# Narrow products in the recurrence levels and an early first expert in a one-core layer with attention, recurrence and experts

## The reference

```python
def hgrn_block(q, k, v, logf, S0):
    b = jnp.cumsum(logf, axis=1)
    diff = b[:, :, None] - b[:, None, :]
    decay = jnp.exp(jnp.where(causal[None, :, :, None, None], diff, -jnp.inf))
    A = jnp.einsum('bthk,btshk,bshk->bhts', q, decay, k)
    o = jnp.einsum('bhts,bshv->bthv', A, v) + jnp.einsum('bthk,bhkv->bthv', q * jnp.exp(b), S0)
    S_new = jnp.exp(bL)[..., None] * S0 + jnp.einsum('bshk,bshv->bhkv', k * jnp.exp(bL[:, None] - b), v)

def hier_moe(h, w_group, w_router, wg, wu, wd):
    g_sel = jnp.argmax(t @ w_group, axis=-1)
    top_v, top_i = lax.top_k(e_logits_of_the_group, 2)
    gates = p_group * jax.nn.softmax(top_v, axis=-1)
    experts = g_sel[:, None] * 8 + top_i
    # rows are sorted by expert and padded to blocks of 128; for each block xb of expert e:
    #   (silu(xb @ wg[e]) * (xb @ wu[e])) @ wd[e], times the gate, added to the token's row
```

## Time and profile before

| | |
|---|---|
| median of 3 runs | 2820.53 us (2820.53 to 2821.08) |
| the profiled execution | 2819.19 us, span 2817.5 us |
| TensorE busy | 2675.3 us (95%) |
| VectorE, ScalarE, GpSimd busy | 1548.5, 763.4, 713.5 us |
| DMA | 432.73 MB, mean 154 GB/s |
| projection and recurrence | about 10 to 1075 us |
| sample attention, then attention with routing | about 1075 to 1841 us |
| experts | about 1843 to 2817.5 us |

### The profile page before, as it was taken

The page is one execution under the profiler, slowest core; times in us unless marked ns, Lnnn a source line. Parts: engine busy times, 40 slices in busy tenths (PEclk is TensorE's granted clock), DMA queues, the critical chain, the costliest instruction groups (busy, mean ns, idle before and its releaser), DMA issues. The chain is left out here.

```text
span 2817.5 us, 38815 instructions
## 1 busy us (share of the span) xinstructions
PE 2675.3 (95%) x11801; PEld 1605.4 (57%) x11802; DVE 1548.5 (55%) x2861; ACT 763.4 (27%) x2102; POOL 713.5 (25%) x1001
## 2 busy tenths in 40 slices
PE   8999999999999987999999999759999999999996
PEld 6777777767777766455555555424444444444442
DVE  3565665555565565667777767625444444544443
ACT  1222222222222221555565666101111111111111
POOL 2111111111111120112222222133443433434332
PEclk9999999999999998899999999779999999999998
DMA  6000000100000029222212111389998878898883
GB/s 255 31 31 34 26 26 26 41 30 34 26 26 26 30 62 317 95 90 90 90 46 90 46 46 61 95 297 385 389 388 318 325 250 323 326 338 325 295 288 128
DMA packets 233641, 432.73 MB, mean 154 GB/s; under 512 B 31618, under 2 KB 89346, under 8 KB 233552
## 3 DMA queue, kind: packets, MB, share of 16 engines
q1 hardware_dynamic: 168080, 324.48, 32.2%
q0 software_dynamic: 30768, 94.78, 9.2%
q10 hardware_dynamic: 34704, 12.37, 1.7%
HBM read 324.77 MB, written 94.95 MB: 149 GB/s over the span
## 5 line engine op out<-in xcount | busy, mean ns | idle before, releaser
L673 PE MATMUL z_psum<-w_in_sb,hT 128*128 128x512 f32 x1088 | 482.1, 594 | 0.0
L667 PE MATMUL z_psum<-hT,w_in_sb 128*128 128x128 f32 x3264 | 374.2, 276 | 3.2 <-DMA w_in_sb<-in_w_in 3.2
L667 PEld LDWEIGHTS z_psum<-hT,w_in_sb 128*128 128x128 f32 x3264 | 370.0, 193 | 4.1 <-issue 4.1
L2081 PE MATMUL gate_psum<-w_gate_sb,block_rows_T 128*128 x720 | 318.9, 596 | 21.7 <-DMA w_gate_sb<-in_w_e_gate 21.7
L673 PEld LDWEIGHTS z_psum<-w_in_sb,hT 128*128 128x128 f32 x1088 | 200.4, 190 | 222.0 <-issue 221.0
L2085 PE MATMUL up_psum<-w_up_sb,block_rows_T 128*128 x720 | 316.4, 592 | 1.5 <-DMA w_up_sb<-in_w_e_up 1.5
L2095 PE MATMUL down_psum<-w_down_sb,hidden_T 128*128 x720 | 316.3, 592 | 0.4 <-DVE hidden_T L2003 0.4
L1274 ACT ACTIVATE w_in_sb<-score_psum,neg_max 128x512 f32<-128x512 f32 (+3 forms) x320 | 196.9, 622 | 203.1 <-DVE neg_max L1361 202.8
L310 POOL TENSOR_TENSOR level_decay<-log_decay 128x256 f32<-128x256 f32 x116 | 73.6, 634 | 702.9 <-DVE level_operand L505 702.9
L1948 ACT ACTIVATE square_out<-block_out 128x1024 f32<-128x1024 f32 x45 | 46.2, 1027 | 755.7 <-issue 738.9
L2081 PEld LDWEIGHTS gate_psum<-w_gate_sb,block_rows_T 128*128 128x128 f32 x720 | 137.4, 191 | 195.9 <-issue 195.9
(11 more groups left out here) (308 smaller groups left out, 3425.0 us busy)
## 6 DMA issues: line engine op xcount, KB each, us to landing
w_gate_sb<-in_w_e_gate SPq DMA_DIRECT2D x32, 2048.0 KB, 13.9
w_up_sb<-in_w_e_up SPq DMA_DIRECT2D x32, 2048.0 KB
w_down_sb<-in_w_e_down SPq DMA_DIRECT2D x32, 2048.0 KB, 12.5
w_in_sb<-in_w_in SPq DMA_DIRECT2D x7, 2048.0 KB, 18.7
hidden_by_lane<-hidden ACTq DMA_DIRECT2D x720, 16.0 KB
scratch_z<-z_ring SPq DMA_DIRECT2D x34, 256.0 KB, 2.0
scratch_y<-w_in_sb SPq DMA_DIRECT2D x17, 512.0 KB, 2.6
scratch_h<-h SPq DMA_DIRECT2D x17, 512.0 KB, 2.6
```

Source lines behind the costliest of these rows:

```text
L667: mm = pe.matmul(out[:, hd * P:(hd + 1) * P], w[:, g, c, hd * P:(hd + 1) * P], hT[:, u, c, :], start=(c == 0), stop=(c == DC - 1))
L673: mm = pe.matmul(out[:, :], hT[:, u, c, :], w[:, g, c, :], start=(c == 0), stop=(c == DC - 1))
L2081: mm = pe.matmul(gps[:, :], xT[:, u, c, :], part(wg, slot, c), start=(c == 0), stop=(c == DC - 1))
```

## The change

Levels 2 to 7 of the 16 prompt tiles stream only the 64 late (query) columns of each head; the results lie side by side in the first 64 columns of a head's bank. Level 2 loads 96 columns of weights and is merged by two plain copies of 32 partitions; levels 3 to 7 are merged by a masked copy of half the elements.

The expert stage's gate and up weights, gathered rows and gathered sums now lie in `w_in_sb` and their semaphores live across both stages. Expert 0 is always the first run (a one is written into the presence table). Its gate and up weights are loaded by SP behind the next-to-last tile's rows; the first 128 slots of its queue are read from the table, turned into row numbers on VectorE, and gathered by GpSimd before the stage ends. In `experts` these loads and this gather are gone, and the down weights of run 0 come behind gate and up of run 1. The gates are stored in three pieces: tiles 0 to 13 and the sample tile early, tiles 14 and 15 behind the arrival of the block lists.

```diff
@@ merge
+                if pos == 2 and not is_last(t):
+                    nc.vector.tensor_copy(heads(A[:, :])[0:32, :, 32:64], heads(lps[0][:, :])[0:32, :, 0:32])
+                    nc.vector.tensor_copy(heads(A[:, :])[64:96, :, 96:128], heads(lps[0][:, :])[64:96, :, 32:64]).then_inc(cp_ok, 1)
+                    return
+                if pos > 2 and not is_last(t):
+                    by_half = lambda a: a.rearrange("p h (g s m) -> p h g s m", s=2, m=m)[:, :, :, 1, :]
+                    nc.vector.copy_predicated(by_half(heads(A[:, :])), by_half(mask[:, l:l + 1, :].to_broadcast([P, HEADS, P])),
+                                              heads(lps[pos % 2][:, :])[:, :, 0:64].rearrange("p h (g m) -> p h g m", m=m)).then_inc(cp_ok, 1)
+                    return
@@ level
+                    elif pos == 2 and not is_last(t):
+                        mm = pe.matmul(lps[0][0:96, hd * P:hd * P + 64], left[:, hd * P:hd * P + 96],
+                                       halves_of(right[:, c], 32)[:, :, 1, :], start=True, stop=True)
+                    elif pos > 2 and not is_last(t):
+                        mm = pe.matmul(lps[pos % 2][:, hd * P:hd * P + 64], left[:, c],
+                                       halves_of(right[:, c], P >> pos)[:, :, 1, :], start=True, stop=True)
@@ attend_mix, SP
             store_y(LAST - 1)
             spread_h(LAST - 1)
+            sp.wait_ge(s_ps, FIRST[NU])
+            sp.dma_start(pre["wg"][:, 0, :, :], dr["w_e_gate"].rearrange("l e (c p) f -> (l e) p c f", p=P)[0]).then_inc(pre["g_in"], 16)
+            sp.wait_ge(pv, FIRST[NU])
+            sp.dma_start(pre["wu"][:, 0, :, :], dr["w_e_up"].rearrange("l e (c p) f -> (l e) p c f", p=P)[0]).then_inc(pre["u_in"], 16)
             store_y(LAST)
+            sp.wait_ge(gates_ok, 1)
+            for tiles in EARLY:
+                store_gates(tiles)
             sp.wait_ge(h_ok, TILES)
             sp.dma_start(h2[ORDER[LAST]], h[:, :]).then_inc(h_out, 16)
             sp.wait_ge(h_out, 16 * TILES)
-            sp.wait_ge(gates_ok, 1)
-            with nc.allow_non_contiguous_dma(reason="two gates for a token"):
-                sp.dma_start(dr["gates"][0:2 * TILES * P].rearrange("(t p c) o -> p t (c o)", p=P, c=2), gates[:, :, :]).then_inc(gates_out, 16)
+            sp.wait_ge(sc_out, 32 * TILES)
+            with nc.allow_non_contiguous_dma(reason="slots of the first block, one at a time"):
+                for j in range(LANES):
+                    sp.dma_start(keep["first_slots"][j * SQ:(j + 1) * SQ, :],
+                                 dr["table"][0].rearrange("(i r) o -> r (i o)", r=SQ)).then_inc(first_in, 16)
+            sp.wait_ge(blk_in, 16)
+            sp.wait_ge(gates_ok, 2)
+            store_gates(LATE)
@@ attend_mix, GpSimd, behind the fetch of block_queue_rows
+            pool.wait_ge(first_ok, 1)
+            pool.wait_ge(h_out, 16 * TILES)
+            for i in range(LANES):
+                pool.indirect_dma_start(out=pre["xg"][:, 0, i, :], out_offset=None, in_=dr["h2"].rearrange("t (j d) -> (t j) d", j=LANES),
+                                        in_offset=bass.IndirectOffsetOnAxis(ap=keep["first_rows"][:, i:i + 1], axis=0)).then_inc(pre["x_in"][0], 16)
@@ attend_mix, VectorE
+            chain.after(nc.vector.memset(full[:, 0, 0:1], 1.0))
...
+            dve.wait_ge(first_in, 16 * LANES)
+            chain.after(ts(keep["first_slots"][:, :], keep["first_slots"][:, :], 0.5, -0.25, ALU.mult, ALU.add))
+            ts(keep["first_rows"][:, :], keep["first_slots"][:, :], float(LANES), lane[:, 0:1], ALU.mult, ALU.add).then_inc(first_ok, 1)
             dve.wait_ge(blk_in, 16)
@@ experts, SP
-            gate(0)
-            up(0)
-            down(0)
             gate(1)
             up(1)
+            down(0)
@@ experts, GpSimd
-            gather(0, 0)
+            pool.sem_inc(tok_ok, 1)
             gather(1, 1)
@@ build
+            pre |= {"wg": w[:, 0:3, :, :], "wu": w[:, 3:6, :, :],
+                    "xg": w[:, 6, 4:8, :].rearrange("p c n -> p (c n)").rearrange("p (u i n) -> p u i n", u=2, i=LANES),
+                    "yg": w[:, 6, 0:4, :].rearrange("p c n -> p (c n)").rearrange("p (u d) -> p u d", u=2),
```

57 lines of the change are left out of this document (35 added, 22 removed).

## The result

| | before | after |
|---|---|---|
| median | 2820.81 us (2820.53 to 2821.84, 4 runs) | 2804.34 us (2804.0 to 2806.23, 4 runs) |
| ratio, 95% interval | | 0.9944 [0.9932, 0.9956] |
| span of the profiled execution | 2817.5 us | 2802.3 us |
| VectorE busy | 1548.5 us | 1528.7 us |

The change brings 16.5 us. The forecast was 28.5 (2792, range 2785 to 2802), so the time lies outside the range, on the dear side. The span is 15.2 us shorter. The shift between the two traces (how much earlier the same product starts) splits it at three places: 4.5 us at the end of the last prompt tile, 2.7 at the start of the boundary, 14.3 at the fourth block. The projection stage, with what follows it, thus brought 2.7 of 10.4 in this execution, and boundary and experts 12.5 of 18.1.

The account below looks back on a forecast made before the run. TensorE, busy 95% of the span, was taken to bound the kernel, with the DMA limiting the first expert blocks. Projection 10.4 plus boundary and experts 18.1 gave 28.5 us off, so 2792 us, range 2785 to 2802.

Parts of the forecast that it names:

- 10.4: Projection stage: gain in us from narrowing levels 2 to 7, 3.4 plus 7.0; bounds 3 to 12.
- 18.1: Boundary and experts: gain in us counted by the DMA, from earlier start, fewer loads and gathers, and slack; bounds 14.6 to 21.5.
- Levels 3 to 7: Projection, 16 tiles: 640 narrow passes at 0.106 instead of 0.111 us each, 3.4 us gained; bounds 0 and 34.
- rival C: Projection: narrow passes follow their streamed columns at 0.058 us each, 31 us more gained, 2761 us; chance 0.04.
- Level 2: Projection: shorter passes and copies at 0.2 us each start level 3 0.44 us earlier per tile, 7.0 us in 16 tiles.
- Strided columns (E): Projection: rival that streamed columns picked with a stride make passes slower, decisive from 0.150 us a pass; chance 0.06.
- Stage end: Boundary between routing and experts: earlier lists let the stage end at 1835.4, 5.5 us earlier; bounds 2 to 7.
- Up to this point the weights set the end: Expert stage, to the fifth run's up weights: DMA loads, not TensorE, limit, so 18.1 us counts instead of 20.
- My 2 us for waits for hidden rows: First expert blocks: estimated loss to waits for the block before's hidden rows, taken off TensorE's gain to give 20 us.
- Rival B: First expert blocks: TensorE, not the DMA, limits, so 20 us gained instead of 18.1, 2790 us; chance 0.10.
- Rival D: Expert stage: the preload is paid back, only 5.5 us and the projection stay, 2805 us; chance 0.07.
- Rival A: Boundary: lists come no earlier and GpSimd holds the barrier, none of the 5.5 us gained, 2797.5 us; chance 0.13.

Follow-up runs that it names:

- run 0: Not a follow-up kernel: the expert stage's first run of blocks for one expert, always expert 0 in the changed kernel; no measured time or ratio of its own.
- operand_first: The changed kernel, but VectorE builds level 3's operand ahead of level 2's two copies; 2797.8 us, ratio 0.9924 to the kernel before.
- state_early: The changed kernel, but SP loads the sample states once the last tile's first group of products has ended, not the eighth; 2802.33 us, ratio 0.9928.

## Why the barrier opens late

**gather_behind**: the four gathers of block 0 behind the barrier again, the preloads stay.

```diff
@@ attend_mix, GpSimd
-            for i in range(LANES):
-                pool.indirect_dma_start(out=pre["xg"][:, 0, i, :], ...).then_inc(pre["x_in"][0], 16)
@@ experts, GpSimd
-            pool.sem_inc(tok_ok, 1)
+            gather(0, 0)
```

> The changed kernel, but the four gathers of block 0 stand behind the barrier again, as in the kernel before. Theory G (the barrier in front of the experts doesn't open before GpSimd's indirect transfers, issued just ahead of it, have landed): from the last engine's work to the first instruction behind the barrier 1.9 us instead of 5.4, so the first weight load is issued 2 to 3.5 us earlier; the first product then waits for its own gathers and comes later, at about +12.9 behind the barrier. Rival H (SP's wait for the last gates holds the barrier): the gap from VectorE's last work to the barrier stays as long, 5 us or more.

**late_gates_free**: SP doesn't wait for the gates' stores at the stage's end.

```diff
-            sp.wait_ge(gates_out, 16 * (len(EARLY) + 1))
@@ experts, GpSimd, ahead of gate_of(0, 0)
+            pool.wait_ge(pre["gates_out"], 48)
```

> The changed kernel, but SP doesn't wait for the stores of the gates at the end of the routing stage; GpSimd waits for them in the expert stage ahead of the first use. Theory G: SP's wait was over in time, the barrier still opens 5.4 us after GpSimd's last gather, nothing else moves, same time as the changed kernel (0.9944 of before). Rival H: the gap falls to about 2 us, the first weight load and the first product come 3.4 us earlier.

Timeline of gather_behind:

```profile
1831.62 0.48 DVE L1642 TENSOR_SCALAR block_rows_all<-block_rows_all,lane_number 128x512 uint32<-128x512 uint32 x1
...
1834.05 0.18 POOL L1877 COPY block_tokens<-block_rows_all 128x4 uint32<-128x4 uint32 x1 [9.71 <-issue]
...
1836.25 0.44 SPq L1845 DMA_DIRECT2D w_in_sb<-in_w_e_gate  x1
...
1846.52 9.59 PE L2123 MATMUL gate_psum<-w_in_sb,block_rows_T 128*128 x16 [16.43 <-DVE block_rows_T L2029]
```

Without the gathers the gap is 1834.05-1832.10 = 1.95 us, with them 5.40 (5.36 to 5.64 in all thirteen kernels that have them there and no other load beside them). So theory G holds and H falls: in late_gates_free nothing moved (0.9937 [0.9922, 0.9952]). gather_behind's first product comes 7 us later; its ratio, 0.9957 [0.9942, 0.9972], is the worse one, but the interval overlaps with the changed kernel's. What the barrier waits for is shown by a kernel further down (second_gate_early), which has 2 MB of other traffic beside the same four gathers. Timelines of down_later and, second, of second_gate_early; the last line of each fence is from the table of DMA issues and gives the time from the last gather's issue to its landing (count, us):

```profile
1829.53 0.95 POOL L1294 DMA_INDIRECT w_in_sb<-scratch_h,first_rows  x1 [0.30 <-issue]
1835.90 0.18 POOL L1883 COPY block_tokens<-block_rows_all 128x4 uint32<-128x4 uint32 x1 [5.42 <-issue]
...
w_in_sb<-scratch_h,first_rows POOLq DMA_INDIRECT x1, 2.8
```

```profile
1831.74 0.95 POOL L1296 DMA_INDIRECT w_in_sb<-scratch_h,first_rows  x1 [0.30 <-issue]
1842.02 0.18 POOL L1885 COPY block_tokens<-block_rows_all 128x4 uint32<-128x4 uint32 x1 [9.33 <-issue]
...
w_in_sb<-scratch_h,first_rows POOLq DMA_INDIRECT x1, 6.7
```

Same instructions, and 9.33 us instead of 5.42. So it is not GpSimd's own work that holds the barrier. The last gather lands at 1829.53+2.8 = 1832.3 in the one and at 1831.74+6.7 = 1838.4 in the other, and the first instruction behind the barrier comes 3.6 us later in both. The same 3.6 us stand in all six kernels whose traces have the landing, best_second_gate among them, so what is waited for is the landing of GpSimd's gathers. It is not SP's load. Each engine ends the stage with a drain; by the view of that line in second_gate_early (length in ns three times, then the start) GpSimd's and SP's are:

```profile
L1043 POOLq DRAIN  x1: 12343/12343/12343, 1827.7 to 1827.7; - x1
...
L1043 SPq DRAIN  x1: 7/7/7, 1832.0 to 1832.0; - x1
```

GpSimd's lasts until 1840.0, 1.6 us behind the last landing. SP's takes 7 ns while SP's own load moves until 1839.3 us, so that load only slows the gathers. In the kernel before GpSimd's drain lasted too, from 1825.2 to 1838.4 us with the list fetch in flight, but VectorE ended later, at 1840.88, and hid it.

The Trainium skill ("DMA: Bandwidth & Descriptors", Anatomy of one DMA) gives 2.0 us and 436 GB/s for a transfer that GpSimd issues; by that a gather of 128 KB takes 2.3 us, an estimate. The traces have 2.7 to 3.0 us from issue to landing for the last gather where nothing is beside it, 4.2 to 4.7 for the first, and 6.4 to 8.3 beside the 2 MB, so only the best case comes near.

## Why the first blocks gain so little

Block 2 waits for its gate weights. Three things come there almost together, as the changed kernel's timeline shows (block 2's product starts at 1875.38, see above):

```profile
1856.34 11.22 ACTq L1987 DMA_DIRECT2D hidden_by_lane<-hidden  x16
...
1868.45 0.60 ACT L1980 ACTIVATE silu_gate<-gate_psum 128x512 f32<-128x512 f32 x1 [19.18 <-issue]
...
1873.65 0.69 DVE L2043 TENSOR_TENSOR hidden<-up_psum,silu_gate 128x512 f32<-128x512 f32 x1
```

Block 1's gate product ends at 1863.6, but ScalarE is issuing block 0's 16 transfers until 1867.6 and makes block 1's exponential at 1868.45. VectorE's hidden rows, for which block 2 waits too, come at 1874.3; the weights at 1875.1. The repairs were tried alone and together.

**down_later**: SP's first loads behind the barrier.

```diff
             gate(1)
             up(1)
+            gate(2)
+            up(2)
             down(0)
-            with sp.Fori(2, last + 1) as r:
+            down(1)
+            with sp.Fori(3, last + 1) as r:
```

> The changed kernel, but SP loads gate and up of run 2 ahead of the down weights of run 0 (gate 1, up 1, gate 2, up 2, down 0, down 1). Theory (block 2 waits 4.9 us for its gate weights because 2 MB that are needed only 16 us later lie in front, and then runs at 1.2 GHz for 3 us): the wait goes, the clock stays up, the end comes 5 to 8 us earlier: 2797 to 2800. Rival (the DMA as a whole sets the pace of the first blocks, as the prediction had it): the wait moves to the down weights of run 0 or to block 3, and the end stays within 2 us: 2802 to 2806.

**exp_inside**: ScalarE.

```diff
             gate(0)
-            spread_a(0, 0)
-            act.dma_start(fw[:, :], ...)
+            spread_a(0, 0, range(11))
             gate(1)
+            spread_a(0, 0, range(11, 16))
+            act.dma_start(fw[:, :], ...)
```

> The changed kernel, but ScalarE issues 11 of the 16 transfers of block 0's hidden rows, then makes the exponential of block 1, then the other 5. Theory (block 2 has two limits: its gate weights, landed 36 us after the stage's first load, and the hidden rows of block 1, which wait for ScalarE behind 10.8 us of DMA issues): alone this gains nothing, since the weights still come at the same time: within 1 us of the changed kernel, block 2 still waits 4.9 us. Rival (ScalarE's queue is the limit in this kernel): block 2 starts 2.5 us or more earlier.

**exp_and_down**: both.

> The changed kernel with both: gate and up of run 2 ahead of the down weights of run 0, and block 1's exponential ahead of the last 5 transfers of block 0. Theory: block 2's wait falls from 4.9 (3.6 with the loads alone) to about 1.0 us, as at block 1, and its gate product takes 7.0 us instead of 10: from block 0's first product to block 2's up product 39 us instead of 46, the end 6 to 7 us earlier than in the changed kernel: 2797 to 2799. Rival (the DMA limits again as soon as both are gone): some of it comes back as waits for weights in blocks 3 and 4, over 2 us.

**gate2_first**: as down_later, but in the order gate 1, up 1, gate 2, down 0, up 2, down 1.

> The changed kernel, but SP issues gate 1, up 1, gate 2, down 0, up 2, down 1, gate 3: only the gate weights of run 2 move, one place. Theory (three limits within 2 us): the wait of block 2 is no longer ended by the DMA and falls from 4.9 to 3.4 to 3.8 us, where the hidden rows of block 1 end it; the DMA keeps 370 GB/s or more from 1860 to 1890; the end comes 1 to 3 us earlier. Rival (the DMA as a whole is the limit): waits for weights return in blocks 3 and 4, the end stays.

**two_hidden**: exp_inside, and block 1's hidden rows in memory of their own (half of `fo[:, 1]`, with a semaphore for their transfers), so that they needn't wait until block 0's have been read.

> The changed kernel with ScalarE's exponential of block 1 ahead of the last 5 transfers of block 0, and the hidden rows of block 1 in memory of their own. Theory: VectorE has block 1's hidden rows 1 us after its up product, but block 2 still waits for its gate weights, 4.5 to 4.9 us, and still runs at 1.2 GHz: same end as the changed kernel within 1 us. Rival (the hidden rows alone held block 2): it starts 3 us earlier.

**three_limits**: gate2_first and two_hidden together.

> The changed kernel with both edits. Theory: block 2 waits 1.0 to 1.5 us and its gate product takes 7.0 to 7.1 us; from block 0's first product to block 3's gate product 53 us instead of 59.9. The weights of block 4 had landed 5.4 us ahead of their use in the changed kernel, so of these 6.9 us about 5.4 to 6.5 reach the end: 2798 to 2799. Rival (DMA): under 2 us reach the end, and block 3 or 4 waits for weights.

**second_gate_early**: three_limits, and expert 1's gate weights before the barrier too.

```diff
@@ attend_mix, SP
             store_gates(LATE)
+            sp.wait_ge(pre["g_in"], 16)
+            sp.dma_start(pre["wg"][:, 1, :, :], ...[1]).then_inc(pre["g_in"], 16)
@@ attend_mix, VectorE
-            chain.after(nc.vector.memset(full[:, 0, 0:1], 1.0))
+            chain.after(nc.vector.memset(full[:, 0:2, 0:1], 1.0))
@@ experts, SP
-            gate(1)
             up(1)
             gate(2)
```

> three_limits, and the gate weights of expert 1 are loaded by SP before the barrier too, behind the last gates (DMA at 21 to 51 GB/s there). Theory (the DMA work in front of block 2's up weights): they land 37 to 38 us after the stage's first load instead of 42.7, TensorE wants them at 38.6, so there is no wait over 1.1 us in the first blocks and no stretch at 1.2 GHz behind block 0; the end comes 5 to 7 us earlier than with three_limits, 2797 to 2799 (ratio 0.991 to 0.992). The barrier may open up to 1 us later, since the gathers share the DMA. Rival (each wait that goes makes room for the next): block 3 or 4 waits for weights, 3 us or more, and the end stays within 2 us of three_limits.

| kernel | ratio | block 2: wait, start to start of its gate product | waits for weights after that | block 0's first product to block 3's |
|---|---|---|---|---|
| before | | 1.1, 7.0 us | 0 | 57.6 us |
| after | 0.9944 | 4.9, 10.0 | 0 | 59.9 |
| down_later | 0.9937 [0.9923, 0.995] | 3.6, 8.7 | 0.2 | 57.2 |
| exp_inside | 0.994 [0.9925, 0.9956] | 4.6, 10.0 | 0 | 59.4 |
| exp_and_down | 0.9944 [0.993, 0.9957] | 3.3, 8.7 | 2.8 in block 4 | 56.4 |
| gate2_first | 0.9936 [0.9921, 0.9951] | 4.3, 8.7 | 0 | 58.7 |
| two_hidden | 0.9939 [0.9924, 0.9954] | 3.8, 8.7 | 0 | 57.5 |
| three_limits | 0.9937 [0.9923, 0.995] | 1.0, 10.9 | 3.8, block 2's up weights | 59.4 |
| second_gate_early | 0.9933 [0.992, 0.9947] | 1.0, 7.0 | 0 | 52.9 |

(In all of them block 0's own gate product starts behind the long wait and takes 8.7 to 10.0 us. In three_limits the 10.9 us contain the wait for the up weights; the up product behind it takes 9.7.)

None of the single repairs moves the end by more than the intervals, and the table says why. With the weights alone moved (down_later, gate2_first), the wait is ended by the hidden rows: the releaser is no DMA any more, and the product starts 0.2 us behind them. gather_behind shows the same by chance: its weights for block 2 land 15 us ahead, and the hidden rows alone make it wait 3.7 us. With the hidden rows alone repaired (two_hidden), it is still the weights'. exp_and_down shows two further limits at once. VectorE was ready to write block 1's hidden rows when the up product ended, at 1871.4, but waited on until block 0's transfers had landed, since both use one buffer (its timeline):

```profile
1873.83 0.69 DVE L2048 TENSOR_TENSOR hidden<-up_psum,silu_gate 128x512 f32<-128x512 f32 x1 [4.07 <-DMA hidden_by_lane<-hidden]
```

And its order of loads made a hole in the DMA: `down(1)` stands in SP's queue until `down(0)` has landed, and all loads behind it with it. The table by stretch has 318 GB/s where the changed kernel has 376, and two waits of 1.4 us for weights come back in block 4. Table by stretch, and TensorE's waits from 1860 to 1935 us, of exp_and_down:

```profile
1875.00:1890.00 15.00, 15.00 (x32) 6.48 (x32) 5.50 (x5) 0.60 (x1) 4.00 (x5) 0.89 0.88 318
```

```profile
PE gate_psum L2131 <- issue: 3.3, 1, 3.3
PE up_psum L2135 <- DMA w_in_sb<-in_w_e_up: 1.4, 1, 1.4
PE gate_psum L2131 <- DMA w_in_sb<-in_w_e_gate: 1.4, 1, 1.4
```

With all three limits gone block 2 starts after 1.0 us, and then its up product waits. Timeline of three_limits:

```profile
1871.65 7.13 PE L2139 MATMUL gate_psum<-w_in_sb,block_rows_T 128*128 x16 [1.01 <-issue]
...
1882.54 2.92 PE L2143 MATMUL up_psum<-w_in_sb,block_rows_T 128*128 x3 [3.76 <-DMA w_in_sb<-in_w_e_up]
```

These weights arrive 41.4 to 42.8 us after the stage's first load in after, gate2_first, two_hidden and three_limits alike. That is the DMA's amount of work in front of them, and second_gate_early bears it out: with 2 MB less in front they arrive 35.4 us after it, there is no wait over 1.0 us and no stretch at half the clock behind block 0, and the first blocks take 52.9 us, as expected, 6.5 less than in three_limits. But the barrier, with 2 MB beside the gathers, opens 3.9 us later, not the 1 us that I allowed. The end gains 1 to 2 us, within the interval, where I expected 5 to 7. So here the rival was right in the end, by a mechanism that neither theory had.

**all_repairs**: exp_and_down, operand_first and state_early.

> The changed kernel with the operand of level 3 ahead of level 2's copies, the early load of the sample states, and both repairs of block 2. Theory (four separate losses, which add): 4 + 3 + 6.5 us under the changed kernel, 2790 to 2792, 1.1% under the kernel before. Rival (they overlap, since the DMA sets the pace of blocks 3 and 4): no faster than 2794.

Measured 2796.91 us, 0.9912 [0.9898, 0.9925], not the 2790 to 2792 that I expected. By the traces the DMA's hole and the shared buffer leave the expert part where it was, and only the projection's repairs count; operand_first alone had 0.9924.

**best**: three_limits, operand_first and state_early.

> three_limits with the operand of level 3 ahead of level 2's copies and the early load of the sample states. Theory: 6.5 us more from the projection stage, 2791 to 2793, 1.0 to 1.1% under the kernel before. Rival: no more than three_limits.

Measured 2798.13 us, 0.9917 [0.9903, 0.993], so no better than all_repairs, and 5 us or more above the 2791 to 2793 that I expected.

**best_second_gate**: best and second_gate_early.

> The same on top of best. Theory: 5 to 7 us under best, 2791 to 2793 (ratio 0.989 to 0.990). Rival: within 2 us of best, 2796 to 2799.

Measured 2793.82 us, between theory and rival; ratio 0.9903 [0.9888, 0.9919] to the kernel before, which was 2820.55 beside it: 27 us, and its interval lies wholly under that of the changed kernel, so it is faster than that one, and the fastest kernel here by the medians (all_repairs' and best's intervals overlap with its own). By the tile period 3.8 us of its lead over the changed kernel are operand_first's. Which share the other edits have isn't shown.

## Why the prediction was wrong, point by point

- **Levels 3 to 7: 3.4 us forecast, 0.7 measured.** The eight passes took the 0.84 us that the forecast had. The step that failed is to take 0.106, a mean over a whole group, as the pace of one pass, and to count it as gained. The prediction had the pace beside it, 0.111 between the logits' weight loads, and set it aside. Only the first pass of a narrow group is shorter, which is also why the logits' 16 passes average 0.106; and the first pass of the wide group behind is longer by the same 0.05. Something measured from start to start is worth something only if the next start moves. (The sum as written, 640 x 0.005, gives 3.2.) That the weight load and not the streamed columns sets the pace stood up: rival C (0.058 a pass) and the 81 ns of the Trainium skill ("TensorE: Matmul & The Clock Gate", Back-to-back issue gap) aren't seen.
- **Level 2: 7.0 forecast, 4.0 measured.** TensorE's part was right (0.24 a level against 0.22). The step that failed is the price of the copies, 0.2 each; they took 0.28 and 0.29, in sum what the masked copy had cost. I scaled the operand's halves (256 elements, 0.41) by the elements. The trace of before had the better row in level 1's copy from the same memory; from its 256 elements in 408 ns and these 128 in 278, some 150 ns would be fixed (an estimate: a fixed part and the same time for each element). The Trainium skill ("VectorE: DVE Perf Modes", The TRN2 errata, on the fixed extra latency per instruction) has 120 cycles and one an element, at 0.96 GHz, for a source in PSUM: 258 ns for 128, an estimate by its figures. The trace agrees to 8 and 12%; by it the two copies would have stood at 0.52, and of the 3.8 us that they were to bring 1.9 would have been left.
- **Strided columns (E)**: no cost down to every second element; eight passes of level 7, like those of level 4, take 0.84 us. That agrees with the Trainium skill ("SBUF — State Buffer", Door 1).
- **Stage end: 5.5 forecast, 2.9 measured.** The lists, the gates in pieces and the gathers all went as fast as forecast or faster. The failed step is the 1.93 us from the last work to the barrier's opening, which I took over from the earlier trace rows without asking what GpSimd had in flight there: before the list fetch, which VectorE outlasted, now four gathers, and the barrier opens 3.6 us behind the landing of the last.
- **"Up to this point the weights set the end": failed.** The DMA's side of the sum was well sized: the fifth block's up weights landed 1940.43-1921.09-2.66 = 16.7 us earlier against 17.7. But TensorE, which I had at 20, made 11.6: the first product 13.9 instead of 15.7, and then 2.3 us lost where I expected 4.3 gained. The old waits of 3.80 and 1.52 us went as forecast, but a 1.02 stands at block 1 and block 2's wait grew from 1.06 to 4.86, so the waits together are only 0.5 shorter. The half clock behind block 2's wait cost 3.0, and the prediction has no term for it, though its own rows show a granted clock of 0.68 around the boundary. My 2 us for waits for hidden rows had no queue behind them; ScalarE's 16 transfers, 10.2 us, were in the trace of before, hidden under the wait for weights.
- **Rival B** was right that TensorE and not the DMA limits there, and wrong in its price: it kept TensorE's 20 us and would end at 2790.
- **The tail** gave 0.9 us back, which I hadn't counted: from the last product to the end it is 1.7 shorter, and the wait in front of the last product is 0.7 longer. Why is open.
- **Rival D** gave almost the right time (2805) for the wrong reason: it kept all 10.4 us of the projection, and waits of over 10 us in blocks 1 to 4 did not come. That is luck. Rival A named the right place: GpSimd holds the barrier. It had the reason wrong, and its sign didn't come: counted from the last scatter (1821.61 and 1820.14) the barrier opens 4.1 us earlier, not under 3.

In sum, by the two traces (28.5 forecast, 15.2 found): 7.7 too much for the projection (5.7 of it by the tile periods, 2.0 lost between the last prompt tile and the boundary), 2.6 for the stage end, 3.9 for the first blocks, less the tail's 0.9. The range was too narrow on the dear side: the low bound for the boundary, 14.6, came from the lists alone and 12.5 were found, and of the projection's low bound of 3 only 2.7 reached the boundary.

## What to carry to other kernels

When a load or wait that covered the first rounds of a loop is removed, lay out for each of these rounds every input with its own queue (here weights, exponential, shared buffer, and again weights, all within 4 us), since repairing one shows the next. Count an instruction's pace as a gain only together with the instruction behind it. And whoever issues GpSimd's transfers ahead of a barrier should take the barrier as waiting for their landing, which other traffic delays.

## What the runs showed of the hardware

- A barrier behind GpSimd's indirect transfers opened 1.95 us after the last work without them, 5.36 to 5.64 us after the last issue with four of 128 KB in flight, and 9.1 to 9.33 us with 2 MB of another load beside them; counted from the last gather's landing, it was 3.6 us in all six kernels whose traces have the landing. GpSimd's drain at the stage's end took 2.9, 8.4 and 12.3 us in the three cases, SP's 7 ns.
- TensorE's granted clock fell to 1.2 GHz behind waits of 3.3 to 5.0 us at block 2's gate product in eleven kernels, and of 3.8 at its up product in two (8.5 to 10.0 us to the next start instead of 7.0), and not behind waits of 1.0 us or one of 2.5 in all_repairs. In the kernel before, a wait of 3.80 us at block 1 cost nothing, while waits of 3.17 to 3.34 at the same place in the three kernels with only levels changed cost 1.5 to 1.6. At the sample tile 1.90 to 1.98 us brought the half clock in three kernels, and 2.27 and 2.87 didn't in two. So the length of the wait alone doesn't tell; what does stays open.
- Eight TensorE passes with 128 columns of weights each load these every 0.111 us, with 128 streamed columns as with 64; with 96 columns of weights every (0.67-0.16)/6 = 0.085 us, close to the 0.084 that the prediction took.
- On VectorE a copy of 32 partitions by 128 elements out of PSUM takes 278 to 289 ns, one of 64 partitions by 256 takes 408, a masked copy of 128 by 256 takes 444 and of 128 by 512 takes 736 (medians).
